# Differential attention: variance step off VectorE, first head's loads spread over slots, value products with 128 weight columns

## The reference, cut to what matters

```
sc = q k^T * scale            # two maps m = 0, 1 per head
p  = softmax(where(allowed, sc, -inf))
a  = p[:, :, 0] - lam * p[:, :, 1]
o  = a @ v                    # v has 64 columns per head
y  = rmsnorm(o, g_subln) * (1 - lambda_init)     # mean of o*o over 64 columns, + 1e-6
```

## Time and profile before

| | us |
|---|---|
| median of 3 runs | 1988.22 (1986.01 to 1991.34) |
| profiled execution, its own time | 1992.78 |
| profiled execution, span from first to last instruction | 1991.0 |
| mean granted TensorE clock in it | 0.959 |

### The profile page before, as it was taken

How to read it: one execution, slowest core, us unless ns; L and a number is a source line. 1 busy time by engine, 2 the same in 40 slices (tenths; PEclk the granted TensorE clock), 3 DMA queues, 4 the chain that set the end, 5 groups by cost and what they waited for, 6 DMA issues and landing times.

```text
span 1991.0 us, 34303 instructions
## 1 busy us (share of the span) xinstructions
PE 1846.0 (93%) x11552; PEld 1557.2 (78%) x11552; DVE 1305.7 (66%) x2685; ACT 1079.7 (54%) x2406; POOL 604.8 (30%) x542
## 2 busy tenths in 40 slices
PE   6999999799999999999999999998789999979998
PEld 6999999677777778787878887776566666657886
DVE  7704888357777777777777764444577777854454
ACT  6421112256767666666666653343578888961221
POOL 0000000034444444444444431102246566650000
PEclk9999999699999999999999899999699999999999
DMA  6433222200101010100001013324600422025442
GB/s 220 109 72 106 68 68 84 74 6 7 27 5 26 5 26 5 26 10 21 19 13 26 6 38 108 111 84 131 139 1 29 92 62 56 9 88 209 170 148 85
DMA packets 121837, 129.05 MB, mean 65 GB/s; under 512 B 81936, under 2 KB 94992, under 8 KB 120464
## 3 DMA queue, kind: packets, MB, share of 16 engines
q1 hardware_dynamic: 121744, 127.86, 22.2%
HBM read 85.89 MB, written 41.94 MB: 64 GB/s over the span
## 4 chain that ended last, share of the span: by engine, by line
PE 73%; DVE 13%; issue 6%; ACT 5%; DMA 1%; POOL 1%; SPq 0%; DVEq 0%; ACTq 0%; POOLq 0%
PE ps L666 9%; PE ps L620 6%; PE ps L652 6%; PE ps L621 5%; PE ps L622 5%; DVE small L1509 4%; PE ps L607 4%; PE ps L609 4%; PE ps L608 4%; PE ps L898 3%; PE ps L900 3%; PE ps L899 3%; PE ps L640 3%; PE ps L641 3%; PE ps L849 3%
## 5 line engine op out<-in xcount | busy, mean ns | idle before, releaser
L1627 POOL TENSOR_TENSOR ring_r<-ring,sp_hi 128x512 fp32r<-128x512 f32 (+1 forms) x320 | 359.7, 1124 | 810.7 <-DVE sp_hi L1391 810.7
L666 PEld LDWEIGHTS ps<-v,ring 128*128 128x128 f32 x2176 | 288.5, 195 | 62.1 <-issue 27.3
L666 PE MATMUL ps<-v,ring 128*128 128x65 f32 x2176 | 291.1, 274 | 19.8 <-ACT ring L1048 12.3
L1036 ACT ACTIVATE ring<-ps 128x512 f32<-128x512 f32 (+1 forms) x320 | 170.3, 532 | 213.6 <-PE ps L641 128.1
L1388 DVE SCALAR_TENSOR_TENSOR ring<-ring,ps 128x512 f32<-128x512 f32 (+1 forms) x320 | 192.0, 600 | 44.3 <-ACT ring L1041 41.6
L1653 POOL TENSOR_TENSOR p<-p 128x1024 f32<-128x1024 f32 (+4 forms) x96 | 164.6, 1726 | 164.3 <-ACT p L1158 164.0
L607 PE MATMUL ps<-w_hl,ht_hi 128*128 128x256 f32 x768 | 212.8, 277 | 0.7 <-DVE w_hl L1246 0.6
L608 PE MATMUL ps<-w_hl,ht_hi 128*128 128x256 f32 x768 | 212.6, 277 | 0.0
L609 PE MATMUL ps<-w_hl,ht_lo 128*128 128x256 f32 x768 | 212.6, 277 | 0.0
L620 PE MATMUL ps<-ht_hi,w_hl 128*128 128x512 f32 x448 | 200.8, 448 | 8.5 <-DVE sb_s L1418 7.8
L1509 DVE TENSOR_REDUCE small<-ps 128x1 f32<-128x1024 f32 (+4 forms) x192 | 168.8, 906 | 48.8 <-PE ps L807 28.7
(11 more groups left out here) (182 smaller groups left out, 3934.6 us busy)
## 6 DMA issues: line engine op xcount, KB each, us to landing
w_raw<-in_w_narrow SPq DMA_DIRECT2D x18, 512.0 KB, 3.8
xb<-in_x SPq DMA_DIRECT2D x16, 512.0 KB, 3.9
gate_scr<-ring SPq DMA_DIRECT2D x64, 128.0 KB, 1.8
cs<-rot_scr SPq DMA_DIRECT2D x32, 256.0 KB, 3.8
gb<-gate_scr SPq DMA_DIRECT2D x16, 512.0 KB, 3.8
yb<-y_scr SPq DMA_DIRECT2D x16, 512.0 KB, 4.7
xr<-in_x SPq DMA_DIRECT2D x16, 512.0 KB, 4.3
out_y<-ob SPq DMA_DIRECT2D x16, 512.0 KB, 2.9
```

The costliest lines, as they stand in the source:

```text
L666: mm = pe.matmul(ps[:, 4 + i % 2, j * (HD + 1):(j + 1) * (HD + 1)], ring[:, 4 + i % 2, j * P:(j + 1) * P], v1[:, kb, :], start=True, stop= ...
L1627: nc.gpsimd.tensor_tensor(ring_r[:, i % 4, j0 * P:], ring[:, i % 4, j0 * P:], sp_hi[:, i % 4, j0 * P:].bitcast(F32), ALU.subtract).then_in ...
```

## The change

VectorE's `ss/64 + eps` (L1563) is gone. ScalarE's Ln now reads the sum itself, with scale 1/64 and a bias column `eps_col` that VectorE fills once at the start, and waits for the sum. GpSimd makes the same variance for its Newton step, as the first instruction of `df_norm`. VectorE's sum waits for the earlier Ln and the earlier variance instead.

The value products take two neighbouring key blocks as weights: `v[:, kb:kb + 2, :]`, 128 columns. The result fills 128 partitions of bank 7; partitions 64 to 127 hold products with the next block and are never read. The last block needs a neighbour, so both value tiles get one more block, which GpSimd clears after the memory stage; TensorE waits for that once. For the same reason the values tile becomes a flat one, viewed with 65 columns per block in the stick-breaking stage and with 64 in the differential one, and the constants `cst` move into a part of `ring` that is free at the start.

`load_df_v(0)` moves one slot up, ahead of the waits and of that slot's successor's store; `load_qk(0)` is issued in four parts of three DMAs, in slots 28, 29, 30 and 31, each after its slot's stores. Counts of DMAs and bytes are unchanged.

```diff
-        v1 = sb("v1", [P, SB, HD + 1], F32)
+        v_flat = sb("v_flat", [P, (SB + 1) * HD], F32)
...
-                v2 = sb("v2", [P, SB, HD], F32, a)
+                v2 = sb("v2", [P, SB + 1, HD], F32, a)
...
+        v1 = v_flat[:, 0:SB * (HD + 1)].rearrange("p (k d) -> p k d", d=HD + 1)
+        v_even = v_flat[:].rearrange("p (k d) -> p k d", d=HD)
+        cst = ring[:, 4:6, :].rearrange("p a b -> p (a b)")[:, 0:5 * P].rearrange("p (c q) -> p c q", c=5)
...
+                if slot == X_SLOT[-1] + 2:
+                    load_df_v(0)
                 if slot == X_SLOT[-1] + 3:
                     for u in range(2):
                         sp.wait_ge(qk_out[u], 32 * NT // 2)
                     sp.wait_ge(x_pj, len(X_ITEMS))
-                    load_qk(0)
-                    load_df_v(0)
+                if 3 <= slot - X_SLOT[-1] < 7:
+                    load_qk(0, ((0, 2 * DQ), (0, 0), (1, 2 * DQ), (2, 0))[slot - X_SLOT[-1] - 3])
...
+                if G == 0:
+                    pe.wait_ge(v_end, 2)
...
-                    v = v2[:, kb, :] if h % 2 else v1[:, kb, 0:HD]
-                    mm = pe.matmul(ps[0:HD, 7, o0:o0 + P], v, at[:, G % 3, n * P:(n + 1) * P], start=(kb == 0), stop=(kb == row))
+                    v = (v2 if h % 2 else v_even)[:, kb:kb + 2, :]
+                    mm = pe.matmul(ps[:, 7, o0:o0 + P], v, at[:, G % 3, n * P:(n + 1) * P], start=(kb == 0), stop=(kb == row))
...
-                rsqrt_of(df_tmp(4, 4), df_tmp(8, 4), df_tmp(12, 4), df_var, s // 2 + 1, df_ln, df_y0)
+                b = s // 2
+                act.wait_ge(df_ss, b + 1)
+                if b:
+                    act.wait_ge(df_nr, 4 * b)
+                nc.scalar.activation(df_tmp(8, 4), df_tmp(0, 4), ACT.Ln, scale=1.0 / HD, bias=eps_col).then_inc(df_ln, 1)
+                act.wait_ge(df_ln, b + 1)
+                nc.scalar.activation(df_tmp(12, 4), df_tmp(8, 4), ACT.Exp, scale=-0.5).then_inc(df_y0, 1)
...
+            nc.vector.memset(eps_col, EPS).then_inc(eps_ok, 1)
...
                 dve.wait_ge(df_sq, b + 1)
+                if b:
+                    dve.wait_ge(df_var, b)
+                    dve.wait_ge(df_ln, b)
                 nc.vector.tensor_reduce(ss, osq[:], AXX, ALU.add).then_inc(df_ss, 1)
-                dve.wait_ge(df_ss, b + 1)
-                if b:
-                    dve.wait_ge(df_nr, 4 * b)
-                nc.vector.tensor_scalar(var, ss, 1.0 / HD, EPS, ALU.mult, ALU.add).then_inc(df_var, 1)
...
+            pool.wait_ge(m_y, N_MT)
+            for v in (v_even, v2):
+                nc.gpsimd.memset(v[:, SB, :], 0.0).then_inc(v_end, 1)
...
+                pool.wait_ge(df_ss, b + 1)
+                nc.gpsimd.tensor_scalar(var, df_tmp(0, 4), 1.0 / HD, EPS, ALU.mult, ALU.add).then_inc(df_var, 1)
+                pool.wait_ge(df_var, b + 1)
                 pool.wait_ge(df_y0, b + 1)
-                pool.wait_ge(df_var, b + 1)
```

More of the change, by code:

```diff
@@ L157, in build @@
         minus_lam = small[:, 1:2]
+        eps_col = small[:, 7:8]
         qk_scale = sb("qk_scale", [P, 1], F32)
@@ L183, in build @@
                 gpre_b = sb("gpre_b", [P, D], F32, a)
-                cst = sb("cst", [P, 5, P], F32, a)
             with ExitStack() as a:
@@ L308, in build @@
         pool_go = sem("pool_go")
+        v_end = sem("v_end")
+        eps_ok = sem("eps_ok")
         lam_ch, lam_e = sem("lam_ch"), sem("lam_e")
@@ L327, in _ @@
                 sp.sem_inc(one, 1)
-            sp.dma_start(cst[:], const_sq.rearrange("c p q -> p c q")).then_inc(const_in, 16)
+            sp.dma_start(cst, const_sq.rearrange("c p q -> p c q")).then_inc(const_in, 16)
             sp.dma_start(small[:, 0:1], const_col).then_inc(const_in, 16)
@@ L439, in store_qk, with load_qk @@
                 sp.dma_start(qk_scr[h, 1, :, cols], lo_tmp[:, f % 2, :].bitcast(F32)).then_inc(qk_out[f % 2], 16)
-            def load_qk(h):
+            def load_qk(h, only=None):
                 u, half = h % 2, S // 2
                 for part, dst, row, first in ((0, df_k, 2 * DQ, 0), (0, df_q, 0, half), (1, df_k, 2 * DQ, half), (2, df_q, 0, 0)):
+                    if only not in (None, (part, row)):
+                        continue
                     cols = slice(first, first + half)
@@ L451, in load_df_v @@
             def load_df_v(h):
-                dst = v2[:] if h % 2 else v1[:, :, 0:HD]
+                dst = (v2 if h % 2 else v_even)[:, 0:SB, :]
                 sp.dma_start(dst, v_rows[h + SB_H]).then_inc(df_v[h % 2], 16)
@@ L1190, in df_root @@
                     return
-                rsqrt_of(df_tmp(4, 4), df_tmp(8, 4), df_tmp(12, 4), df_var, s // 2 + 1, df_ln, df_y0)
+                b = s // 2
[5 more added lines that the diff above has]
+                nc.scalar.activation(df_tmp(12, 4), df_tmp(8, 4), ACT.Exp, scale=-0.5).then_inc(df_y0, 1)
             act.wait_ge(m_y, N_MT)
+            act.wait_ge(eps_ok, 1)
             for u in range(2):
@@ L1556, in df_variance @@
                 b = s // 2
-                ss, var = df_tmp(0, 4), df_tmp(4, 4)
+                ss = df_tmp(0, 4)
                 dve.wait_ge(df_sq, b + 1)
+                if b:
+                    dve.wait_ge(df_var, b)
+                    dve.wait_ge(df_ln, b)
                 nc.vector.tensor_reduce(ss, osq[:], AXX, ALU.add).then_inc(df_ss, 1)
-                dve.wait_ge(df_ss, b + 1)
-                if b:
-                    dve.wait_ge(df_nr, 4 * b)
-                nc.vector.tensor_scalar(var, ss, 1.0 / HD, EPS, ALU.mult, ALU.add).then_inc(df_var, 1)
             for u in range(4):
```

## The result

| | before | after |
|---|---|---|
| median of 7 runs each, us | 1992.29 (1986.01 to 1998.66) | 1979.22 (1975.79 to 1981.04) |
| ratio, 95% interval | | 0.9934 [0.9914, 0.9954] |
| profiled execution, its own time | 1992.78 | 1980.99 |
| span | 1991.0 | 1978.8 |
| mean granted TensorE clock | 0.959 | 0.959 |

The account below looks back on a forecast made before the run. Even slots were held by TensorE with ScalarE right behind, odd ones by ScalarE's wait for VectorE's variance. Gains of 18.3, 4 and 2 us made 24.3, taken from the median 1988.2: 1964 us, range 1951 to 1976.

Parts of the forecast that it names:

- The differential stage: The whole sum, from the end of the memory stage to the end: 24.3 us less.
- The 24 middle slots: Full slots of the differential stage, 1479.64 to 1742.40 us: 18.3 us gain, from 10.95 to 10.2 us per slot.
- Slots 2 to 5: Early differential slots, 50.3 us, led by TensorE at a partly low clock and by padding memsets: 4 us gain.
- what follows slot 29: After 1742.4 us: one odd slot and ten more groups, less 0.4 us on GpSimd: 2 us gain.
- The variance: Removing VectorE's L1563 ends ScalarE's wait, 12.2 us in 12 odd slots; bounds 1.0 and 2.1 us per odd slot.
- The cover named for it: GpSimd's 88.8 us of waiting for ScalarE hides its added 0.4 us in every second slot, except at the end.
- Rival (a): Differential stage: only the variance pays, the gaps stay or lie under other waits; 15 us gain, 1973; chance 0.15.
- The value products: TensorE loses 1.25 us of gaps per slot; records at 0.112 us instead of 0.108 add 0.1 per slot.
- Rival (c): Value products: 128-column weight loads set the pitch; at 0.195 us +20, 2008; decides from 0.176; chance 0.04.
- The loads: Memory stage: same bytes and issues, moved between stores; taken at 0, bounds −2 and +2 us.
- The 6.12 us stall: Memory stage: VectorE held 6.12 us by GpSimd's memset; not touched by the change, so still there.
- rival (d): TensorE waits more for ScalarE, its clock falls more often; some 14 slots eat the gain: 1986; chance 0.05.

Follow-up runs that it names:

- experiments 1: The changed kernel with 16 unused floats behind the flat values tile, making the shift of later tiles 0 modulo 256 bytes: 1966.26 us, ratio 0.9874.
- experiment 2: The kernel before with only the constants moved into `ring` and 48 unused floats (192 bytes) behind `v1`: 2001.59 us, ratio 1.0045.
- experiment 4: The kernel before with only the variance edit (L1563 gone, Ln from the sum, GpSimd's own variance): 1978.47 us, ratio 0.9934.
- experiment 5: The kernel before with only the 128-column value products, plus a gap keeping later tiles at their place: 1981.67 us, ratio 0.9945.
- experiment 6: The kernel before with only the loads of the first differential head moved between the stores: 1992.94 us, ratio 0.9998.

## Why the prediction was wrong, point by point

**The step that failed** is one that the prediction doesn't have: it put the cost of the flat values tile and of the moved constants at nothing, without a sentence. Its sum ends "24.3 us", counted only between 1429 us and the end, on the ground that "all three edits act between the end of the memory stage and the end of the differential stage". The declarations of the tiles act on all that lies behind them: +12.8 us in a loop that ended at 345 us and 1.6 ahead of it, shown by experiments 1 and 2. With the place undone the ratio is 0.9874; the forecast, 1963.9 over 1988.2, was 0.9878. That the two are so close is partly luck: the interval is 4 us wide on either side, and the memory stage of that trace is 5 us shorter for no forecast reason.

**The differential stage.** Forecast −24.3, measured −25.4 (profiled executions). The 24 middle slots take 243.59 us, 10.15 each (forecast 10.2), and ScalarE is busy for 233.07 of them, 96% (forecast: over 95%). Slots 2 to 5 went from 50.3 to 46.5 us (forecast −4), and what follows slot 29 from 51.5 to 49.1 (forecast −2). That ScalarE is late next was right; the split was not. The text said odd ones near 10.2 and even ones near 9.8 to 10. It had read the even slots from one of 9.92 us, while the twelve in the middle stretch average 10.5 before the change. Now they are 11.1 us in the mean with ScalarE full (10.99 of 10.99 above), and odd ones 9.2, from 11.4. A pair of slots is the unit in which this pipeline can be forecast, a single slot isn't.

**The variance.** GpSimd's new instruction takes 0.19 us (0.20 forecast), its next follows 0.21 behind:

```profile
1604.42 0.19 POOL L1680 TENSOR_SCALAR small<-small 128x4 f32<-128x4 f32 x1
...
1604.82 0.20 POOL L1684 TENSOR_TENSOR small<-small 128x4 f32<-128x4 f32 x1 [0.21 <-POOL small L1680]
```

The cover named for it was there: GpSimd still waits 62.2 us for ScalarE, and ScalarE's wait for the variance isn't in the view any more. Nor is TensorE's wait for VectorE's copy, as was said; in the 24 slots before it stood there with 14.8 us:

```profile
PE ps L833 <- DVE at L1540: 14.8, 12, 1.5
```

In the waits of the changed kernel from 1492 to 1740 ScalarE waits 6.9 us for minima (8.1 before) and 2.7 for transposes (4.1):

```profile
POOL p L1674 <- ACT p L1169: 62.2, 37, 4.1
...
ACT p L1160 <- DVE small L1532: 6.9, 10, 1.1
...
ACT at L1179 <- PE ps L842: 2.7, 8, 0.6
```

The forecast had taken half of these two as gone, 6.1; 2.6 went. The middle slots gained 19.2 us all the same where 18.3 were forecast, so ScalarE's idle time went elsewhere too; no run separates that.

Rival (a), "only the variance pays", was priced at 15; alone it gave 0.66% or 13 us (experiment 4), and the columns alone 0.55% (experiment 5), so (a) was wrong, and that the time came out nearest to it (1973 forecast, 1979 measured) is chance.

**The value products.** 0.112 per record was right: successive value records start 0.112 us apart at the median in the changed kernel and 0.109 before. The 0.17 us ahead of the group and behind it are gone:

```profile
1608.37 0.52 PE L842 MATMUL ps<-ident,p 128*128 128x128 f32 x3 [0.41 <-ACT at L1179]
1608.72 0.83 PE L860 MATMUL ps<-at,v 128*128 128x128 f32 x6
1609.37 0.38 PE L816 MATMUL ps<-df_k,df_q 128*128 128x256 f32 x1
```

Here it is 0.65 us from the first of six records to the scores after them, 0.108 each, with no gap. Before, eight records took 1.02, 0.16 more than 8 x 0.108. That it hangs on 64 against 128 columns is shown by experiment 5, where nothing else of TensorE's order changed. The Trainium skill's rule that a change of tiling mode drains TensorE agrees (TensorEngine Tiling (Array Packing), Key Properties). Rival (c) needed a pitch of 0.176 or more; it is 0.11, although the loads themselves take 193 to 199 ns in the mean (experiment 5). The Trainium skill's rule that a load overlaps matmuls in flight only when the row groups differ (TensorE: Matmul & The Clock Gate, Part 3, The mechanism) doesn't agree with that pitch.

**The loads** at 0 ± 2: right for the time, by experiment 6. The memory stage is 2.6 us shorter in the profiled pair, but it is 2.7 shorter in experiment 2 as well, where its loads are as before; so that need not be theirs. The 6.12 us stall was still there, as said (1396.01, 6.12). **The clock** fell no more often: 0.959 before and after, so rival (d) has no part in it. Its price was also added up wrong: 14 slots at 1.7 us on top of 1963.9 are 1988, not 1986.

**What would have found it:** comparing the byte offsets of the tiles in the two compiled programs. The diff says it in one line, 1040 floats become 1088. But the kernel before alone has no row with a price for it. The honest term would have been a bound, worked out from the 2304 records of the loop and the rows where L607's pitch isn't 0.113: in a stretch around 230 us of the kernel before it is 0.118, and 2304 x 0.005 is 11.5 us. That would have carried the range to 1976 + 11.5.

## What to carry to other kernels

A tile whose size changes moves all tiles behind it, and that can cost or give more than the edit in a stage that nobody looks at: cut both traces at the same events of the whole span, not only around the edit, and undo the shift with an unused gap before judging the edit itself. Where a tuned loop of matmuls fills TensorE, try some distances between its loaded and its moving operand, which costs a line each. And where a small VectorE instruction takes as long as the GpSimd instruction beside it, change its form before moving it to another engine.

## What the runs showed of the hardware that was not expected

- The pitch of matmuls with 128 weight columns and 256 moving f32 columns depends on where the tiles of the two operands lie to each other: 114.5 to 115.3 ns in the mean at a distance of 64 bytes modulo 256, 118 to 119 at 32, 96 and 192, 120.1 at 0, at a granted clock of 1.00. In this kernel's loop that is 12.8 us, 0.6% of the time.
- At the good distance a pass of 384 records has one pitch from its start to its end, 0.113 or 0.118 us (in the kernel before 0.113 around 200 us and 0.118 around 230). What decides between them is open.
- Four one-column instructions of VectorE beside a GpSimd addition take 4 x 144 ns, one four-column instruction 1.9 to 2.1 us at the median.
- The granted clock is 0.50 (1.2 GHz) after the last projections whether VectorE is held by the memsets or not. What else brings it down there wasn't tried.
